# A decoder stack in fp32r products on one core: where retention's values are centred, how two column sums are formed, and when four feed-forward pieces are made

## The reference, cut to what matters

```python
# after layers 0 and 1
gate = jax.nn.sigmoid(rms_norm(x, ple_norm_g[i]) @ ple_w_gate[i])
x = x + (p[i] @ ple_w_proj[i]) * gate

# retention: rv = h @ w_v, four heads of 128 values
ret = bidirectional_retention(rq, rk, rv, log_decay(ret_decay_fwd), log_decay(ret_decay_bwd))
def head_group_norm(y, gain):
    mu = jnp.mean(y, axis=-1, keepdims=True)
    var = jnp.mean(jnp.square(y - mu), axis=-1, keepdims=True)
    y = (y - mu) * lax.rsqrt(var + EPS)

# feed-forward
x = x + jnp.square(jax.nn.relu(h @ w_up)) @ w_down
```

## Time and profile before

| | us |
|---|---|
| median of three runs | 2417.39 |
| lowest and highest of them | 2416.08, 2418.39 |
| the profiled execution, its own time | 2415.05 |
| its span, first to last instruction | 2413.2 |
| PE busy in it | 2366.2 |
| DVE, ACT, POOL busy | 1623.3, 1062.4, 956.4 |

### The profile page before, as it was taken

The page is one execution under the profiler, slowest core; times in us unless marked ns, Lnnn a source line. Parts: engine busy times, 40 slices in busy tenths (PEclk is TensorE's granted clock), DMA queues, the critical chain, the costliest instruction groups (busy, mean ns, idle before and its releaser), DMA issues.

```text
span 2413.2 us, 31633 instructions
## 1 busy us (share of the span) xinstructions
PE 2366.2 (98%) x11580; PEld 1875.5 (78%) x11580; DVE 1623.3 (67%) x2017; ACT 1062.4 (44%) x1625; POOL 956.4 (40%) x535
## 2 busy tenths in 40 slices
PE   9999999999999999999999999999999999999997
PEld 6888658887777777777788777888877888788885
DVE  6999974467656466476866555455688777648985
ACT  5556562335544545446342333223254434444334
POOL 2899933323222122222232111312345555465553
PEclk9999999999999999999999999999999999999999
DMA  3111333221111111111122111221126665876763
GB/s 137 44 44 52 113 131 122 78 96 45 44 42 39 40 40 45 40 40 41 52 88 76 40 40 32 81 79 36 53 114 162 152 161 149 242 290 233 273 249 122
DMA packets 112116, 238.76 MB, mean 99 GB/s; under 512 B 42360, under 2 KB 45304, under 8 KB 111992
## 3 DMA queue, kind: packets, MB, share of 16 engines
q1 hardware_dynamic: 73040, 216.28, 27.7%
q10 hardware_dynamic: 38952, 20.76, 3.8%
HBM read 184.44 MB, written 46.27 MB: 96 GB/s over the span
## 4 chain that ended last, share of the span: by engine, by line
PE 80%; DVE 8%; issue 4%; ACT 3%; POOL 3%; DMA 1%; ACTq 0%; SPq 0%; DVEq 0%; POOLq 0%
PE ps_A L883 23%; PE ps_B L883 22%; PE ps_B L1410 8%; PE ps_A L1410 8%; PE ps_C L1410 4%; PE ps_D L1410 2%; POOL ta L795 1%; PE ps_C L903 1%; PE ps_B L1156 1%; PE ps_C L1048 1%; POOL accp L795 1%; PE ps_D L983 1%; PE ps_D L1048 1%; PE ps_D L1141 1%; PE ps_D L1129 1%
## 5 line engine op out<-in xcount | busy, mean ns | idle before, releaser
L769 POOL CAST w_hi<-w_raw 128x1024 fp32r<-128x1024 f32 x98 | 108.2, 1104 | 1067.6 <-PE ps_A L883 519.7
L762 POOL TENSOR_TENSOR w_lo<-w_raw,w_hi 128x1024 fp32r<-128x1024 f32 x124 | 305.1, 2461 | 49.7 <-ACT w_hi L1550 41.9
L848 POOL TENSOR_TENSOR down_w_lo<-d_raw,down_w_hi 128x512 fp32r<-128x512 f32 x112 | 178.4, 1613 | 141.3 <-ACT down_w_hi L2238 141.3
L883 PE MATMUL ps_A<-HA_hi,w_hi 128*128 128x512 f32 x640 | 201.2, 396 | 4.3 <-POOL w_lo L762 2.2
L883 PE MATMUL ps_B<-HA_hi,w_hi 128*128 128x512 f32 x640 | 202.5, 398 | 2.7 <-POOL w_lo L762 1.4
L883 PE MATMUL ps_A<-HA_lo,w_hi 128*128 128x512 f32 x640 | 197.6, 390 | 0.0
L883 PE MATMUL ps_B<-HA_lo,w_hi 128*128 128x512 f32 x640 | 197.4, 390 | 0.0
L883 PE MATMUL ps_A<-HA_hi,w_lo 128*128 128x512 f32 x640 | 197.4, 390 | 0.0
L883 PE MATMUL ps_B<-HA_hi,w_lo 128*128 128x512 f32 x640 | 197.3, 389 | 0.0
L883 PEld LDWEIGHTS ps_A<-HA_hi,w_hi 128*128 128x128 f32 x640 | 117.1, 188 | 30.0 <-issue 4.2
L883 PEld LDWEIGHTS ps_B<-HA_hi,w_hi 128*128 128x128 f32 x640 | 116.8, 188 | 30.1 <-POOL w_lo L762 2.7
(11 more groups left out here) (502 smaller groups left out, 5952.2 us busy)
## 6 DMA issues: line engine op xcount, KB each, us to landing
w_raw<-w_dram SPq DMA_DIRECT2D x124, 512.0 KB, 3.3
d_raw<-w_dram SPq DMA_DIRECT2D x64, 512.0 KB, 4.4
t_raw<-u_dram SPq DMA_DIRECT2D x56, 512.0 KB, 6.0
a_raw<-w_dram SPq DMA_DIRECT2D x32, 512.0 KB, 7.5
u_dram<-b SPq DMA_DIRECT2D x56, 256.0 KB, 5.0
u_dram<-t SPq DMA_DIRECT2D x48, 256.0 KB, 6.8
X<-x_dram SPq DMA_DIRECT2D x16, 512.0 KB, 7.2
d_raw<-w_dram SPq DMA_DIRECT2D x32, 256.0 KB, 3.0
```

The source lines that it names most:

```text
L762: pool.tensor_tensor(w_lo[q][:, :, :], w_raw[q][:, :, :], w_hi[q][:, :, :].bitcast(F32), ALU.subtract).then_inc(S[f"w_ready{q}"], 1)
L769: pool.tensor_copy(w_hi[q][:, :, :], w_raw[q][:, :, :]).then_inc(S["w_rounded"], 1)
L848: pool.tensor_tensor(lo[:, :, :], d_raw[i % 3][:, down_parts(x), :], hi[:, :, :].bitcast(F32), ALU.subtract).then_inc(S["down_split"], 1)
L883: op = pe.matmul(AB[b][:, cols], wt[:, w0 + k, :], act[:, k, cols], start=(first and k == ks[0] and step == 0), stop=(last and k == ks[-1] ...
```

## The change

Four edits:

1. **Late pieces.** `t_pieces_after` gives pieces 52 to 55 at items 50 to 53 instead of 48 to 51.
2. **Values centred through their weights.** DVE subtracts from each row of a values' weight tile the mean over the head's 128 columns, in `w_raw`, before POOL splits it (`centre_weights`: a `tensor_reduce` and a `scalar_tensor_tensor` for each of two tiles, twice). The first call stands in the neighbourhood's last pass, ahead of `evacuate(rqT)`; the second behind `evacuate(rqT)` of the second pass. POOL waits for `w_centred` ahead of its split of a values' tile; its one loop is cut into a loop, six pairs written out, and a loop. `centred_turn` becomes `value_turn`, eight transposes; the matrix `centre` goes.
3. **Keys' turn.** It moves from ahead of the first gate's tile to ahead of that tile's k-part 2.
4. **Two column sums.** In both gated sides `norm_stats` is replaced by `split_stats`: ACT rounds `ssum` to `sum_hi`, DVE subtracts to get `sum_lo`, and PE adds over the partitions with an fp32r matrix of ones, four 128x512 fp32r products. The other two openings call `norm_stats` as before, now in the caller.

```diff
         def t_pieces_after(i):
-            return [i + PAIRS] if i < ITEMS + PAIRS else []
+            if i < ITEMS:
+                return [i + PAIRS]
+            return [i + PAIRS - 2] if ITEMS + 2 <= i < ITEMS + 2 + PAIRS else []
...
+            for pair in range(W_TILES["ret"] // 2):
+                for q in range(2):
+                    if pair % 3 == 1:
+                        pool.wait_ge(S["w_centred"], pair // 3 * 2 + q + 1)
+                    split_weights(q)
...
+            def split_stats():
+                n.next("ssum_added", KT)
+                pe.wait_ge(S["sum_split"], n.next("sum_split"))
+                b = take_cd()
+                for i, part in enumerate((sum_hi, sum_lo)):
+                    op = column_sums(part, ones_r, b, i == 0, i == 1)
+                op.then_inc(S["stats_done"], 1)
...
-                centred_turn(v_in[0])
-                pe.wait_ge(S["rk_ready"], n.next("rk_ready"))
-                turn(lambda c: chunk(rkT, c), BLOCKS)[1].then_inc(S["k_turned"], 1)
-                bg = linear(0, HB)
+                value_turn(v_in[0])
+                def turn_keys(k):
+                    if k == 2:
+                        pe.wait_ge(S["rk_ready"], n.next("rk_ready"))
+                        turn(lambda c: chunk(rkT, c), BLOCKS)[1].then_inc(S["k_turned"], 1)
+                bg = linear(0, HB, pre=turn_keys)
                 evacuated(bg ^ 1)
-                centred_turn(v_in[1])
+                value_turn(v_in[1])
...
+            def round_sum():
+                act.wait_ge(S["ssum_added"], n.now("ssum_added"))
+                act.copy(sum_hi[:, :], ssum[:, :]).then_inc(S["sum_hi"], 1)
...
+            def split_sum():
+                after("sum_hi")
+                dve.tensor_tensor(sum_lo[:, :], ssum[:, :], sum_hi[:, :].bitcast(F32),
+                                  ALU.subtract).then_inc(S["sum_split"], 1)
...
+            def centre_weights(i):
+                for q in range(2):
+                    mean = w_mean[:, q, :]
+                    dve.wait_ge(S[f"w_loaded{q}"], 16 * ((RET_AT + 6 * i) // 2 + 2))
+                    step(dve.tensor_reduce(mean, w_raw[q][:, :, :], AX.X, ALU.add))
+                    dve.scalar_tensor_tensor(w_raw[q][:, :, :], mean.unsqueeze(2).to_broadcast([P, KT, P]), -1.0 / P,
+                                             w_raw[q][:, :, :], ALU.mult, ALU.add).then_inc(S["w_centred"], 1)
...
                     normalise(u)
+                if j == PAIRS - 1:
+                    centre_weights(0)
                 if j + 1 < PAIRS:
```

More of the change, by code:

```diff
@@ L240, in build @@
         ones = rm.take("ones", [P, P])
+        ones_r = rm.take("ones_r", [P, P], F32R)
         ident = rm.take("ident", [P, P])
@@ L243, in build @@
         eps = rm.take("eps", [P, 1])
+        w_mean = rm.take("w_mean", [P, 2, KT])
         free0 = rm.spans[0][0]
@@ L249, in build @@
         ta = rt.take("ta", [P, T])
+        sum_lo, sum_hi = (Region(nc, (at, at + 4 * KB)).take(name, [P, T], F32R)
+                          for name, at in (("sum_lo", free0), ("sum_hi", free0 + 4 * KB)))
         def col(name, k=0, n=1):
@@ L386, in build @@
         TAB_X, TAB_Z = RET_HEADS * P, 2 * RET_HEADS * P
-        centre = rr.take("centre", [P, P])
         lg = rr.take("lg", [P, 4, RET_HEADS])
@@ L833, in _ @@
                 n.next(f"lin_done{q}", W_TILES["conv_in"] // 2)
-            with n.loop(pool, (MLP_AT - W_TILES["conv_in"]) // 2 - 1, w_loaded0=16, w_loaded1=16, lin_done0=1,
+            with n.loop(pool, (RET_AT - W_TILES["conv_in"]) // 2 - 1, w_loaded0=16, w_loaded1=16, lin_done0=1,
                         lin_done1=1, w_rounded=2):
+                split_weights(0)
+                split_weights(1)
+            for pair in range(W_TILES["ret"] // 2):
[3 more added lines that the diff above has]
+                    split_weights(q)
+            with n.loop(pool, (MLP_AT - RET_END) // 2, w_loaded0=16, w_loaded1=16, lin_done0=1, lin_done1=1,
+                        w_rounded=2):
                 split_weights(0)
@@ L915, in opening @@
                 n.next("h_ready", KT)
-                norm_stats()
             for b in range(2):
@@ L1034, in gated_side @@
                 opening(0, h)
+                split_stats()
                 linear(1, h)
@@ L1256, in _ @@
             opening(0, HA)
+            norm_stats()
             linear(1, HA)
@@ L1303, in chunk, with value_turn @@
                 return t[rows, c * P:(c + 1) * P]
[L1305 to L1311, removed]
+            def value_turn(v):
+                turn(lambda c: chunk(v, c), BLOCKS)[1].then_inc(S["v_turned"], 1)
             def chunk_states(h):
@@ L1567, in _ @@
             act.wait_ge(S["ssum_added"], DVE_SQUARES - 1)
+            act.wait_ge(S["ones_loaded"], 16)
+            act.copy(ones_r[:, :], ones[:, :])
             act.dma_start(dw_sb[:, :, :], dw).then_inc(S["vec_loaded"], 16)
@@ L1690, in gated_side @@
                     act.dma_start(side_sb[q][:, :], side_dram[layer, q]).then_inc(S[f"side_loaded{q}"], 16)
+                round_sum()
                 norm_stats()
@@ L2529, in gated_side @@
             def gated_side(name, h, side_sb):
+                split_sum()
                 clear_sum()
@@ L2904, in decay_args @@
             def decay_args():
-                dve.scalar_tensor_tensor(centre[:, :], ones[:, :], -1.0 / P, ident[:, :], ALU.mult,
-                                         ALU.add).then_inc(S["centre_ready"], 1)
                 after("gamma_ready", 2)
@@ L3018, in _ @@
                     evacuate(rqT[:, :], 0)
+                    centre_weights(i + 1)
                 for h in range(2):
```

## The result

The changed kernel takes **2403.52 us** (median of 5 runs, 2402.67 to 2405.63); the kernel before, measured beside it, 2416.62 (2415.94 to 2418.39). The ratio is 0.9945, 95% interval 0.9934 to 0.9956: 13.1 us less where 10.9 were forecast. The profiled execution took 2402.84 us with a span of 2401.0, 12.2 less than the span of before, and this 12.2 can be followed place by place.

What follows compares the result with a forecast made beforehand. PE bounds the kernel, busy 2366.2 of 2413.2 us. Retention 5.2, column sums 1.6 and late pieces 4.1 make 10.9 us, so 2417.39 - 10.9 = 2406.5 us (chance 0.70); 8-in-10 range 2403.5 to 2412.5.

Steps and rivals of the forecast that it cites:

- Retention, 5.2: Retention on PE: cheaper value turns and the later keys' turn save 3.3 us in pass one, 1.9 in pass two.
- Centring at no cost: Retention's weight centring on DVE: costs nothing, hidden by 5.7 us of cover at POOL's reader, 3 in the worse order.
- The far price of 3.42 for a pass: Centring on DVE: far end for one 128x1024 pass, 3.42 us as beside POOL's subtraction, where 1.22 was taken.
- Column sums, 1.6: Both gated sides: each column sum falls from 1.72 to 0.94 us on PE, 0.78 saved each, 1.6 for both.
- the rounding of the ones matrix at the start: Start of the kernel: one small operation ahead of a wait for PE; no cost counted.
- Late pieces, 4.1: Items 48 to 55: moving the pieces removes PE's stops there, saving 4.1 us, bounds 2.9 to 4.2.
- the sum itself: Whole kernel: 5.2 + 1.6 + 4.1 = 10.9 us saved, every microsecond counted to the end.
- One for one: Retention with DVE late: take-out, table loads, `decay_args` and rotated keys go late by the same time, and PE stands.
- the handover rival: Keys, second side's sum and item 51 late: 1.5 + 1.0 + 1.3 us lost, about 7 gained, 2410.3 us; chance 0.12.
- the rival of a late DVE: Centring delays the queries' evacuation: keys 6.3 us late, bank 3.6, gain 4.9, 2412.5 us; chance 0.07, 0.04 of it slower.
- the clock: Retention: TensorE falls to the lower clock behind the turns, 11 us tiles take 22; two give 2428 us; chance 0.01.
- the forecast's own best, 2406.2: Whole kernel: the median in us if all terms come at their best; the forecast's other bound was 2410.5.

Runs made afterwards that it cites:

- e9: Changed kernel with eight idle reductions (9.7 us in all) ahead of the first centring on VectorE: 2416.08 us, ratio 0.9996 to the kernel before.
- e14: Kernel before plus only the rounding of the ones matrix on ScalarE at the start, with its wait: 2420.56 us, ratio 1.0015.
- e15: Changed kernel with the fifth up-weight buffer moved another 576 bytes and 18 more waits on ScalarE at the start: 2403.62 us, ratio 0.9943 to before.
- e1: Kernel before with the late pieces alone (prepared two items later): 2412.47 us, ratio 0.9979.
- e8: Changed kernel with the late pieces prepared one item earlier (items 49 to 52): 2407.23 us, ratio 0.9957 to the kernel before.
- e4: Kernel before with only 576 unused bytes ahead of its working region: 2415.89 us, ratio 0.9994.
- e5: Kernel before with the fifth up-weight buffer moved by 64 bytes, the tiles behind it by 1024: 2414.94 us, ratio 0.9989.
- e7: Changed kernel with the keys' turn back ahead of the gate's tile (k-part 0): 2409.30 us, ratio 0.9967 to the kernel before.
- e6: Kernel before with the work tiles behind the fifth up-weight buffer moved by 64 bytes, that buffer left in place: 2415.73 us, ratio 0.9993.
- e12: Kernel before with 512 unused bytes where the change puts its fp32r ones matrix, no instruction more: 2415.91 us, ratio 0.9995.

## Why the prediction was right or wrong

- **Retention, 5.2:** right in each term (3.4 and 1.8): 0.79 to 0.97 per turn, 0.1 for the split tile, the keys 0.39 ahead of PE where 0.36 was worked out. That a turn costs 0.85 rested on an identical instruction in the trace, and held.
- **Centring at no cost:** right. The cover was 4.6 where 5.7 was worked out: where the two subtractions meet, POOL's was the late one, not DVE's. e9 found the end of the cover where the rows of the changed kernel put it. The far price of 3.42 for a pass was not needed.
- **Column sums, 1.6:** the term itself is right (0.7 to 0.8 each). The step "the rounding of the ones matrix at the start is one small operation ahead of a wait for PE" failed: its duration is harmless, its place in ScalarE's stream costs 0.7 (e14, e15). The net is 0.9.
- **Late pieces, 4.1:** 4.2. The cause named on ACT is confirmed: e1 cures it alone, and e8 shows the transfer as the next bound. The cover of item 51 was enough.
- **The step that failed** is the sum itself: "Against the profiled execution: 2415.05 - 10.9 = 2404.15" adds up the four edits and puts all else at nothing, without a reason. But the two new tiles move every address behind them, and that is worth 1.6 us in the up stage (e4, e5), while the instructions added on ScalarE cost 0.7 where attention begins (e14, e15). The first stands in the diff, since `free0` is `up_w4`'s address. With both the sum is 10.9 + 1.6 - 0.7 = 11.8 for a measured 12.2 between the two profiled executions. Of the 3.0 between 2406.5 and 2403.5, 1.3 are the 12.2 less the 10.9 (0.9 of it these two terms, the rest small steps), 0.8 comes because the median of before was 2417.39 when forecast and 2416.62 beside the result, and 0.9 is what the medians differ by beyond the profiled pair, which no run explains.
- **The rivals:** none came. "One for one" for a late stop was too cheap: a stop of 2.4 cost 4.1 and one of 5.3 cost 8.1. By e7, keys two late would have cost nearly double what the handover rival took for them. In the rival of a late DVE the queries' bank is 3.3 late by its own rows (1529.4 + 1.22 less 1527.32), not 3.6; nothing hangs on it. For the clock the prediction read a disagreement out of one turn of 0.85 us without a fall; turns that short can't test the rule.
- **The range:** the result, 2403.52, lies 2.7 below the forecast's own best, 2406.2, and at the very edge of the range of 2403.5 to 2412.5. It is inside by luck: the room on that side was the runs' spread and 1.5 for "a shift of the tail", and behind item 55 nothing was gained. All other doubts were about covers; none was given to what an edit does at a distance.

## What to carry to other kernels

Work out a change from an identical instruction in the trace, and count covers: this was right to about a tenth of a microsecond in both passes of retention, at the sums, at the late pieces and for the stop of e7. Then read the diff once more for what it moves without touching it: a new constant ahead of other buffers changes the addresses that TensorE reads, and a new instruction shifts everything behind it on its engine. Where such a shift can be had alone, by padding, time it alone; the traces tell 0.5 us where medians of ten runs can't tell 2.

## What the runs showed of the hardware

- **Where a weight buffer starts changes the pace of fp32r products.** The same twelve products of 128x512 took some 232.9 ns each with the buffer 128 or 640 bytes short of the other four's place, 229.3 at 64 or 576 short, and 227.0 at their place (17 kernels). Moving other tiles did nothing (e6). Other offsets weren't tried, nor were the other four buffers moved, so whether the absolute start counts or the place beside the other buffers is open.
- **What a stop costs depends on the clock behind it.** All kernels have a stop of 1.9 us in the up stage, between 1810 and 1822:

```profile
1817.20 0.50 PE L1410 MATMUL ps_B<-ht_hi,up_w_hi 128*128 128x512 f32 x1 [1.91 <-DVE b L3109]
```

  Behind it the granted clock stays at 1.00 in twelve profiled executions and is at the lower level for some 3 us in e4, e5, e8, e9 and e12, which costs 1.4 to 1.7 us more. Behind the stop of 1.35 in the earlier trace rows no fall is seen, behind 2.44 and 5.31 (e7, e9, one execution each) there is one.
- **Two instructions can cost 0.7 us half a millisecond later** (e14), by a gap of 0.36 in ScalarE's issues that moves with its stream.
- **A reduction of 128x1024 takes 1.21 us**, beside POOL's rounding too, which it doesn't stretch.
